# Mixture-of-experts stage: the down weights' loads issued by the scalar engine on its own hardware queue, the gate/up loads left on SyncE

## What is computed

```python
g_sel = jnp.argmax(g_logits, axis=-1)              # 8 groups
top_p, top_i = lax.top_k(e_prob, MOE_TOPK)         # 2 of the 8 experts of the group
def expert_block(args):
    xb, e = args
    hid = jax.nn.silu(xb @ w1[e]) * (xb @ w3[e])   # w1, w3: 1024 x 256 each
    return hid @ w2[e]                             # w2: 256 x 1024
out = jnp.zeros((n_tok + 1, dm), ys.dtype).at[slot_tok].add(ys)[:n_tok]
```

## Time and profile before

| what | value |
|---|---|
| median of 3 runs | 1647.29 us (1647.06 to 1651.43) |
| the profiled execution's own time | 1647.83 us |
| its span, from first to last instruction | 1646.1 us |
| PE, ACT, POOL busy in the span | 88%, 29%, 37% |
| bytes moved on SP's queue (q1) | 283.37 MB of 300.16 MB |
| bytes moved on ACT's queue (q10) | 0.08 MB |

### The profile page before, as it was taken

One profiled execution on the slowest core, in us unless ns is written; L12 is line 12 of the kernel. 1 busy time (PEld: TensorE's weight loads), 2 busy tenths in 40 slices (PEclk: granted clock), 3 DMA queues, 4 the chain that ended last, 5 costly groups with the idle time before them and its releaser, 6 DMA issues.

```text
span 1646.1 us, 21875 instructions
## 1 busy us (share of the span) xinstructions
PE 1452.9 (88%) x8226; PEld 987.8 (60%) x8226; DVE 415.9 (25%) x1065; ACT 482.6 (29%) x1067; POOL 605.2 (37%) x710
## 2 busy tenths in 40 slices
PE   7999999898999999997988998939998888888881
PEld 6688876676888888885766335624444444444440
DVE  3003047703111011114153122352221111111114
ACT  3326367723322222224452012202221111111111
POOL 4334545443444444443372014312332222222222
PEclk9999999999999999998999999969999999999996
DMA  3322301032222333113121016449999999999964
GB/s 123 113 95 101 116 30 46 22 102 81 81 96 77 117 114 102 65 66 115 51 103 51 0 44 253 179 188 368 397 397 409 403 404 394 391 387 394 388 276 158
DMA packets 91463, 300.16 MB, mean 182 GB/s; under 512 B 12981, under 2 KB 35665, under 8 KB 66817
## 3 DMA queue, kind: packets, MB, share of 16 engines
q1 hardware_dynamic: 83136, 283.37, 45.8%
q0 software_dynamic: 8160, 15.75, 2.7%
q10 hardware_dynamic: 96, 0.08, 0.0%
HBM read 294.94 MB, written 12.62 MB: 187 GB/s over the span
## 4 chain that ended last, share of the span: by engine, by line
PE 64%; DMA 18%; DVE 6%; ACT 4%; SPq 3%; issue 2%; POOL 2%; ACTq 0%; POOLq 0%; DVEq 0%
PE ps L1008 14%; PE ps L1009 13%; PE ps L1010 13%; DMA big<-in_moe_w_dram 9%; PE ps L1414 6%; DMA wring<-in_moe_w_dram 6%; PE ps L1363 4%; PE ps L1440 3%; SPq L631 2%; DMA hT<-in_moe_w_dram 2%; PE ps L1401 1%; PE ps L1191 1%; SPq L638 1%; PE ps L1338 1%; PE ps L1349 1%
## 5 line engine op out<-in xcount | busy, mean ns | idle before, releaser
L476 POOL TENSOR_TENSOR wring_halves<-wring,wring_halves 128x512 fp32r<-128x512 f32 (+1 forms) x259 | 334.6, 1295 | 390.6 <-ACT wring_halves L471 389.8
L471 ACT CAST wring_halves<-wring 128x512 fp32r<-128x512 f32 (+1 forms) x259 | 158.1, 619 | 445.6 <-PE ps L1010 422.9
L1008 PE MATMUL ps<-wring_halves,big_halves 128*128 128x512 f32 x548 | 218.2, 398 | 21.6 <-POOL wring_halves L476 18.4
L1008 PE MATMUL ps<-hT_halves,wring_halves 128*128 128x512 f32 (+1 forms) x496 | 195.6, 394 | 6.5 <-DVE big_halves L1507 5.3
L1009 PE MATMUL ps<-big_halves,wring_halves 128*128 128x512 f32 (+1 forms) x496 | 195.1, 393 | 0.0
L1010 PE MATMUL ps<-hT_halves,wring_halves 128*128 128x512 f32 (+1 forms) x496 | 194.9, 393 | 0.0
L2168 POOL DMA_INDIRECT y_dram<-xn,sidx x64 | 57.0, 891 | 325.0 <-DVE xn L1929 317.7
L1414 PE MATMUL ps<-big,arena 128*32 128x256 f32 x1024 | 130.3, 408 | 37.9 <-DMA big<-in_moe_w_dram 37.4
L1009 PE MATMUL ps<-wring_halves,hT_halves 128*128 128x512 f32 x372 | 147.7, 397 | 0.0
L1010 PE MATMUL ps<-wring_halves,hT_halves 128*128 128x512 f32 x372 | 147.4, 396 | 0.0
L1008 PEld LDWEIGHTS ps<-wring_halves,big_halves 128*128 128x128 f32 x548 | 104.8, 191 | 48.1 <-POOL wring_halves L476 22.4
(11 more groups left out here) (331 smaller groups left out, 1944.6 us busy)
## 6 DMA issues: line engine op xcount, KB each, us to landing
big<-in_moe_w_dram SPq DMA_DIRECT2D x86, 1024.0 KB, 24.3
wring<-in_moe_w_dram SPq DMA_DIRECT2D x66, 1024.0 KB, 26.6
wring<-in_ffn_w_in_dram SPq DMA_DIRECT2D x22, 1024.0 KB, 7.0
hT<-in_moe_w_dram SPq DMA_DIRECT2D x20, 1024.0 KB, 22.9
wring<-in_fox_w_in_dram SPq DMA_DIRECT2D x7, 2048.0 KB, 8.3
wring<-in_gla_w_in_dram SPq DMA_DIRECT2D x6, 2048.0 KB, 7.9
mkv<-in_moe_w_dram SPq DMA_DIRECT2D x10, 1024.0 KB, 30.2
xn<-in_moe_w_dram SPq DMA_DIRECT2D x10, 1024.0 KB, 30.1
```

Of the source, the lines that this page charges most:

```text
L471: act.copy(hi, src).then_inc(s_hi, 1)
L476: pool.tensor_tensor(lo, src, hi, ALU.subtract).then_inc(s_lo, 1)
L1008: pe.matmul(out, lhs[1], rhs[0], start=start, stop=False)
```

## The change

In the loop over experts 6 to 63 SyncE issues only the gate/up transfers. ACT issues the down transfer of expert e right behind its own copy of the output of expert e - 6 (L954 before, L950 after), on its own queue. The wait on `s_my` that `down_in` had is the one that ACT's copy has already. The first six experts' loads stay where they were, with SyncE. ACT's loop is one round of six shorter, with that round written out, so that the issues end with expert 63; what ACT computes is the same.

```diff
-            def expert(e, j, last):
-                gate_up_in(e, j, last)
-                down_in(e, j, last)
-
             with sp.Fori(1, EXPERTS // E_SLOTS) as it:
                 for j in range(E_SLOTS):
-                    expert(it * E_SLOTS + j, j, it * E_SLOTS + (j + 1 - E_SLOTS))
+                    gate_up_in(it * E_SLOTS + j, j, it * E_SLOTS + (j + 1 - E_SLOTS))
             for e in range(EXPERTS // E_SLOTS * E_SLOTS, EXPERTS):
-                expert(e, e % E_SLOTS, e + 1 - E_SLOTS)
+                gate_up_in(e, e % E_SLOTS, e + 1 - E_SLOTS)
...
+            def down_in(e, j):
+
+                w2 = eslot(j)[1]
+                act.dma_start(w2.rearrange("p k n -> p (k n)"), WW2[e]).then_inc(s_e2[j], 16)
+
-            def block_(base, j, first=False, end=False):
+            def block_(base, j, first=False, end=False, load=True):
                 silu(base + j, j)
                 if not end:
                     xT_out(base + j + 1, j + 1)
                 if not first:
                     y_out(base + j - 1, j - 1)
+                    if load:
+                        down_in(base + (j - 1 + E_SLOTS), (j - 1) % E_SLOTS)
...
-            with act.Fori(1, EXPERTS // E_SLOTS) as it:
+            with act.Fori(1, EXPERTS // E_SLOTS - 1) as it:
                 for j in range(E_SLOTS):
                     block_(it * E_SLOTS, j)
+            for j in range(E_SLOTS):
+                block_(EXPERTS - REST - E_SLOTS, j, load=j <= REST)
             for j in range(REST):
-                block_(EXPERTS - REST, j, end=j == REST - 1)
+                block_(EXPERTS - REST, j, end=j == REST - 1, load=False)
```

## The result

| kernel | median | lowest to highest | runs |
|---|---|---|---|
| before, timed beside it | 1648.25 us | 1646.40 to 1651.43 | 9 |
| after | 1653.67 us | 1651.94 to 1655.80 | 9 |

The ratio is 1.0034, 95% interval 1.0026 to 1.0043: slower by 0.34%; the medians are 5.4 us apart. The forecast was 1651.6 us, inside a range of 1644 to 1660, with "same" as the likeliest and "slower" next; the median lies just beyond the 0.3% that divides the two, and the interval lies on both sides of it. The profiled execution took 1653.05 us, 5.2 more than that of before.

The account below looks back on a forecast made before the run. PE was taken to bound the first experts, the DMA engines about the last forty. 2.3 us won at the start, 2.3 lost again and 4.3 lost at the end: 1647.29 + 4.3 = 1651.6 us, range 1644 to 1660.

Parts of the forecast that it names:

- all weights landed: End of the expert loop's weight traffic: all DMA work ends 2.3 us earlier, at 1602.9 instead of 1605.2 us.
- B(63) against that landing: Last expert's PE block: formerly 2.3 us before the last weights landed, now 4.4 us behind, starting at 1607.3 us.
- three blocks of PE: Loop end: from GU(60)'s landing at 1587.0 us PE is slower than DMA, needing three blocks of 6.75, 20.25 us.
- Issuing costs nothing: ACT's 58 down issues in the expert loop: 0.33 us each, or 2.4 if held, both covered; cost 0.
- the rival that ACT is held: At its issues ACT waits while SyncE is inside one, up to 7.2 us; 30 us if each time; chance 0.11.
- The hole at the start: Idle DMA at 1113 to 1117 us closes as SyncE no longer waits for down products; 2.3 us gained.
- The rate with a second queue: DMA engines' rate in the expert loop: taken as unchanged, 0, with bounds of 21 us lost or gained.
- turns cost: Rival: DMA engines lose time alternating between queues, 2 to 10 us on top of 4.3; 1654 to 1661 us; chance 0.12.
- Which bytes come when: Down transfers overtake gate/up, landing in 7 us instead of 30.7; only 6 MB of gate/up follow GU(60); 4.3 us lost.
- The rival of no overtaking: Both hardware queues are served by age, so the order stays; only the start's gain, -2.3 us, 1645.0 us; chance 0.10.
- PE's first wait two or three experts earlier: Expected sign early in the expert loop: PE first waits for weights two or three experts sooner than before.
- The middle: Expected sign in the middle of the expert loop: blocks of 8.4 to 8.5 us, still 3 MB an expert, no cost.

Follow-up runs that it names:

- e2: Against the kernel before, still one queue: SyncE issues the next expert's gate/up transfer ahead of each down transfer; 1644.27 us, -4.6 us against before.
- e3: Against the changed kernel, two queues: SyncE waits again for the down products after each gate/up pair, its loop written out; 1657.20 us, +8.4 us against before.
- e7: Against the kernel before, one queue: SyncE issues gate/up first, then from DN(36) lets down transfers run ahead as in the changed kernel; 1654.03 us, +5.9 us.
- e5: Against the changed kernel: from DN(35) on, ACT issues down transfers three blocks later, the last one beside GU(63); 1651.40 us, +3.3 us against before.
- e4: Against the changed kernel, streams swapped: ACT issues the gate/up pairs behind its silu, SyncE the down transfers; 1652.90 us, +4.1 us against before.
- e6: Against the changed kernel: from DN(35) on, ACT issues down transfers four blocks later, the last one behind GU(63); 1647.83 us, -0.3 us against before.

## Why the prediction was nearly right

The direction, the mechanism and the place were right; the sum was 1.1 us short of the medians' difference. That it came so near is in part luck, since two terms were off in opposite directions. The profiles give it term by term, from B(2): B(63) came 493.4 - 487.6 = 5.8 us later.

| term | predicted | measured |
|---|---|---|
| all weights landed | -2.3 | 490.9 - 490.0 = +0.9 |
| B(63) against that landing | from -2.3 to +4.4: +6.6 | from -2.4 to +2.5: +4.9 |
| sum | +4.3 | +5.8 |

The luck shows best at GU(60), from which the prediction counts three blocks of PE. It was forecast at 1587.0 us and landed at 1587.1. But the end of the traffic, from which that was worked out, came at 1606.05 and not at 1602.9, and the time from GU(60) to it was 19.0 us and not 15.9. The two errors cancel. What is left is that PE came to B(60) 1.2 us behind the landing, and B(63) so started at 1608.5 instead of 1607.3.

**Issuing costs nothing: right.** L955 takes 0.34 us at 1308.57, and the silu behind it waits for PE alone. SyncE's issues were held longer than before, up to 9.5 us against 7.3, where the prediction had them held less. The group of L631 shows it (duration in ns: least, median, most), and ACT's group below shows that its issues were not held:

```profile
L631 SPq DMA_DIRECT2D big<-in_moe_w_dram x64: 327/1588/9543, 999.7 to 1551.0; - x64
```

```profile
L955 ACTq DMA_DIRECT2D big<-in_moe_w_dram x20: 343/344/369, 1115.1 to 1561.9; - x20
...
DMA to landing us min/median/max: 9.6/10.5/11.5
```

Twelve of ACT's 58 issues fell inside an issue of SyncE's of over 4 us, the longest among them, and took no longer than the others. So the rival that ACT is held fell:

```profile
1345.92 9.54 SPq L631 DMA_DIRECT2D big<-in_moe_w_dram  x1
```

```profile
1348.82 0.34 ACTq L955 DMA_DIRECT2D big<-in_moe_w_dram  x1
```

The lock that the Trainium skill describes (Perfetto Trace Analysis, DMA Instruction — HWDGE) did not show between these two engines: with it, ACT's longest issue would have come near SyncE's.

**The hole at the start: right in place, its worth too large.** SyncE's pair went out at 1112.40 us and the dip is gone. 2.3 us were predicted; the landings say 1.7 on one queue (before to e2, in which nothing else moves the end of the traffic) and 1.4 on two (after to e3). The time of e3 says 3. The share is a mean over 16 engines, while a transfer has landed only when the slowest of them has its part. In e7 the share lost 6.9 us in a hole while the landings went on at nearly their pace and the end moved by 0.7 us, so the engines that set the landings still had work in it. The hole at the start is likely the same in small. No profile here tells the engines apart, so for the start that is not shown.

**The rate with a second queue: the step that failed, 0 taken.** With the same hole, the weights end 490.0 us after B(2) on one queue and 492.3 on two (before, e3). Without the hole it is 488.3 and 489.0 on one (e2, e7), 490.1, 490.1 and 490.9 on two (e5, e4, after). So by the profiles the second queue costs about 2 us of 490, 0.4%. It is the lower edge of "turns cost", a tenth of the upper bound of 21 us. The text had taken the full share of 1.01 for a proof that there was nothing to lose; the share is 1.01 after, too, at 395 instead of 396 GB/s. Single profiles scatter by a microsecond, so this size is an estimate. The times say two things: e6 is 4.3 us slower than e2, but e7, on one queue with the order of after, is no faster than after (+5.9 and +5.4). What in the second queue costs the rate was not tried.

**Which bytes come when: right, its sizes off.** The rival of no overtaking fell at the landing of 10.5 us. The 7 us that the prediction gave a down transfer were too few: DN(63), issued at 1581.40, landed 9.6 us later at 1591.0, 4.0 us behind GU(60), and so what landed after GU(60) was 7 MB, not three gate/up pairs alone. PE passed the DMA engines one block earlier than predicted, at B(59), but only just: from GU(59) to GU(60) the landings are 5.9 us apart, PE's blocks 6.76. So it ended 2.5 us behind the last landing instead of 4.4.

**A part not foreseen: the slow block.** B(58) waited 2.39 us, and then its products took 5.41 us instead of 3.81 at a granted clock of 0.68 in 1572 to 1576 us, part of it at the lower level, 1.2 GHz. In the middle of the loop the next wait for weights takes in such a loss. At B(58) almost all of it was taken in too. Without its 1.6 us PE would have come to B(59) at 1579.9 and stood there until GU(59) landed at 1581.2; it started at 1581.48. So by the landings only some 0.3 us reached the end. In e7 it was different: GU(62) had landed at 1596.8, before B(62) started at 1599.74 behind the slow block, so there the 1.6 us reached the end whole.

**PE's first wait two or three experts earlier: wrong.** It is the wait before B(18) in both, 0.18 us before and 1.88 us after. In after PE stood for gathers before that, 4.3 us up to 1230 us, and was itself later, which the prediction had not counted. It cost nothing in the end, since PE waits for weights after it anyway.

**The middle:** blocks of 8.4 to 8.5 us were right only as a mean; singly they go from 6.76 to 9.96.

That the order at the end is the cause is shown from three sides: e7 makes the loss by it on one queue, e6 undoes it with the change left in place, and e2 turns it to a gain. That the second queue costs some 2 us and the closed hole brings nearly as much is measured less surely.

## What to carry to other kernels

Here the DMA engines bound the loop, and a stream moved to its own queue overtook what stood in the full one. In such a place ask which bytes come last: how much work has the engine left when they land. Put those with the most work behind them first, and let the transfers that are needed late come last; here that was worth 10 us between two orders of the same bytes on one queue (e2 and e7).

A wait in a stream that issues transfers can be taken out by order as well as by another queue, and order costs nothing: e2 has the gain of the start and 4.6 us in all. A full DMA share says that the engines are busy, not that another queue is free. And idle engines in the middle of the loop are worth less than the share says while other engines are behind: by the landings 2.4 us were worth 1.4 (e3), and 6.9 were worth 0.7 (e7).

## What the runs showed of the hardware

**Two hardware queues are served side by side.** ACT's 1 MB transfers landed after 9.6 to 11.5 us while SyncE's took 36 to 41 us at the median; with the small stream gone to a queue of its own the large one's landings became uneven, and PE's longest wait for weights went from 2.5 to 3.6 us. POOL's indirect transfers got slower too, 6.2 to 7.1 us and 5.7 to 6.6.

**A full queue held its engine, SyncE or ACT, and only that engine.** ACT 6.29 us in the row of e4; in after ACT 0.34 us inside an issue of SyncE's of 9.54 us.

**Many long waits cost clock.** From 1230 to 1560 us the granted clock was 0.99 in e2, 0.97 before, 0.95 in after, 0.92 in e6 and 0.91 in e4, and PE's longest wait was 2.3, 2.5, 3.6, 4.2 and 6.4 us. The longest wait alone does not decide it: e7 has one of 12.64 us and 0.97. The rows of e2 and e4:

```profile
1230.00:1560.00 330.00, 271.15 (x1974) 139.48 (x1972) 58.40 (x159) 58.58 (x158) 88.68 (x159) 0.99 1.01 396
```

```profile
1230.00:1560.00 330.00, 283.05 (x1944) 131.16 (x1942) 57.35 (x156) 56.65 (x156) 87.45 (x158) 0.91 1.00 396
```

PE is busy longer in e4 for slightly fewer products (x1944 against x1974), and 396 GB/s are moved in both: where the DMA engines bind, a slower PE costs nothing until its last wait for weights.
